# Two experts' token rows gathered by one indirect transfer and transposed together

## The reference, cut to what matters

```python
weights = g_w[:, None] * softmax(top_vals)        # two experts of one group per token
eid = (g_sel[:, None] * 8 + top_idx).reshape(-1)  # 1024 assignments to 32 experts
...
hid = silu(xb @ w_gate[e]) * (xb @ w_up[e])       # xb: the normalised rows routed to expert e
y   = hid @ w_down[e]                             # 1024 -> 512 -> 1024
...
x = x + sum(y[dest] * weights)                    # back to the tokens
```

## Time and profile before

| | us |
|---|---|
| median of 3 runs | 2028.13 (2027.52 to 2030.19) |
| profiled execution, its own time | 2028.83 |
| its span, first to last instruction | 2027.0 |
| expert matmuls, first and last (tiles large, xF) | 1535.9 and 1999.8 from the span's start |
| busy in the span: PE, DVE, ACT, POOL | 1924.9, 1053.2, 704.8, 57.3 |

### The profile page before, as it was taken

One profiled execution on the slowest core, in us unless ns is written; L12 is line 12 of the kernel. 1 busy time (PEld: TensorE's weight loads), 2 busy tenths in 40 slices (PEclk: granted clock), 3 DMA queues, 4 the chain that ended last, 5 costly groups with the idle time before them and its releaser, 6 DMA issues.

```text
span 2027.0 us, 22190 instructions
## 1 busy us (share of the span) xinstructions
PE 1924.9 (95%) x8902; PEld 1392.4 (69%) x8902; DVE 1053.2 (52%) x1686; ACT 704.8 (35%) x1150; POOL 57.3 (3%) x81
## 2 busy tenths in 40 slices
PE   7999999997999989999999999999998999999997
PEld 6888888775878767888888878877675444444443
DVE  5443544367667886544334446666764333332333
ACT  5321322345545354432222234665652111111111
POOL 0000000100000001000000000000001000000000
PEclk9999999998999999999999999999998999999999
DMA  6333332333222304333333333222189999999996
GB/s 176 95 89 106 96 94 84 71 78 54 70 67 68 109 22 133 95 94 94 94 104 94 94 94 94 76 61 57 32 295 384 406 403 400 406 409 409 409 412 260
DMA packets 260639, 338.92 MB, mean 167 GB/s; under 512 B 10305, under 2 KB 224321, under 8 KB 236977
## 3 DMA queue, kind: packets, MB, share of 16 engines
q1 hardware_dynamic: 254496, 322.28, 46.9%
q0 software_dynamic: 6032, 15.15, 2.2%
HBM read 333.00 MB, written 8.39 MB: 168 GB/s over the span
## 4 chain that ended last, share of the span: by engine, by line
PE 72%; DMA 13%; DVE 9%; ACT 5%; issue 1%; SPq 0%; DVEq 0%; POOLq 0%; ACTq 0%
PE bank L182 70%; DMA large<-w_up 10%; PE bank L185 2%; DMA stage<-w_in 1%; ACT wH L188 1%; ACT p L188 1%; DVE PTL L194 1%; ACT T L188 1%; DVE y L194 1%; DMA xg<-token_rows,tok 1%; DMA stage<-w_r 1%; DVE p L197 1%; DVE score L218 0%; DVE score L200 0%; DVE top L215 0%
## 5 line engine op out<-in xcount | busy, mean ns | idle before, releaser
L182 PE MATMUL bank<-hH,wH 128*128 128x512 f32 x1104 | 438.2, 397 | 21.0 <-DVE stage0L L194 12.0
L182 PE MATMUL bank<-hL,wH 128*128 128x512 f32 x1104 | 431.8, 391 | 0.0
L188 ACT ACTIVATE wH<-stage 128x1024 fp32r<-128x1024 f32 (+3 forms) x238 | 232.5, 987 | 113.0 <-PE bank L182 83.7
L182 PEld LDWEIGHTS bank<-hH,wH 128*128 128x128 f32 x1104 | 209.0, 189 | 68.3 <-DVE stage0L L194 12.0
L182 PE MATMUL bank<-large,xF 128*64 128x512 f32 x1024 | 235.6, 602 | 15.4 <-DMA large<-w_up 14.6
L182 PEld LDWEIGHTS bank<-hL,wH 128*128 128x128 f32 x1104 | 208.9, 189 | 44.3 <-issue 1.9
L182 PEld LDWEIGHTS bank<-large,xF 128*64 128x64 f32 x1024 | 75.0, 138 | 146.4 <-issue 127.8
L182 PE MATMUL bank<-hidH,wH 128*128 128x512 f32 x352 | 137.5, 391 | 2.1 <-DVE stage2L L194 0.9
L182 PE MATMUL bank<-hidL,wH 128*128 128x512 f32 x352 | 137.1, 389 | 0.0
L182 PE MATMUL bank<-large,hF 128*64 128x512 f32 x512 | 116.9, 598 | 1.9 <-DVE hF L194 1.9
L194 DVE TENSOR_TENSOR yoL<-bank,yoH 64x512 fp32r<-64x512 f32 x64 | 44.1, 689 | 110.2 <-ACT yoH L188 109.2
(11 more groups left out here) (480 smaller groups left out, 3356.3 us busy)
## 6 DMA issues: line engine op xcount, KB each, us to landing
large<-w_gate SPq DMA_DIRECT2D x64, 1024.0 KB, 26.9
large<-w_up SPq DMA_DIRECT2D x64, 1024.0 KB, 27.8
large<-w_down SPq DMA_DIRECT2D x64, 1024.0 KB, 27.8
stage<-w_in SPq DMA_DIRECT2D x58, 512.0 KB, 4.3
stage<-w_gate SPq DMA_DIRECT2D x44, 512.0 KB, 3.8
stage<-w_up SPq DMA_DIRECT2D x44, 512.0 KB, 3.7
stage<-w_down SPq DMA_DIRECT2D x16, 512.0 KB, 3.8
gates<-gt POOLq DMA_DIRECT2D x16, 256.0 KB, 4.0
```

The lines of the kernel that those rows point to most:

```text
L182: return self.e.matmul(*a, **k) if self.e is not None else Nothing()
L188: return self.e.activation(*a, **k) if self.e is not None else Nothing()
```

## The change

Gathers are made for two experts at once. The index table has 128 rows and one column for a pair: rows 0 to 63 are the even expert's tokens, rows 64 to 127 the odd expert's. The spare blocks keep a table of their own, `M.tokx`. One indirect DMA fills all 128 partitions of a gather buffer; there are two such buffers instead of three, and only the second waits for `ei` on its first use. A new step `turn_pair` makes eight transposes of 128 by 128 into two PSUM banks (2 and 4), where `turn_x` made eight of 64 by 128 for one expert into bank 2. DVE multiplies by the gain in two operations, one for each bank, and `xF` is kept for four experts. The fetch and the turn of a pair stand at the even `n`; the memory of the third gather buffer is taken by the second `xF` buffer. Weight loads and their order are not edited.

```diff
-        NGR = 3
+        NGR = 2
...
-            M.tok = sb([BLK, NB + NX], I32, "tok")
+            M.tok, M.tokx = sb([128, NB // 2], I32, "tok"), sb([BLK, NX], I32, "tokx")
...
-            for slot in M.xg.slots:
-                slot[1] = ("ei",)
-            M.xF2 = sb([128, 2, 8, BLK], F32, "xF")
-            M.xF = [M.xF2[:, k, :, :] for k in range(2)]
+            M.xg.slots[1][1] = ("ei",)
+
+            late_xF = sb([128, 2, 8, BLK], F32, "xF")
+            M.xF2 = [sb([128, 2, 8, BLK], F32, "xF"), late_xF]
+            M.xF = [M.xF2[k][:, e, :, :] for k in range(2) for e in range(2)]
...
-                add(Step("turn_x", n=n, xg=xg[n], bank=banks.take(("xT", n), 2)))
+                if n < NB:
+                    add(Step("turn_pair", n=n, xg=xg[n], banks=[banks.take(("xT", n, c), at) for c, at in enumerate((2, 4))]))
+                else:
+                    add(Step("turn_x", n=n, xg=xg[n], bank=banks.take(("xT", n), 2)))
...
-            for n in range(2, 2 + NGR):
-                fetch(n)
+            for p in range(1, 1 + NGR):
+                fetch(2 * p)
...
-                if 0 < n < NB - 2:
+                if n % 2 == 0 and 0 < n < NB - 2:
                     turn_x(n + 2)
-                if n + 2 + NGR < NB:
-                    fetch(n + 2 + NGR)
+                    if n + 2 + 2 * NGR < NB:
+                        fetch(n + 2 + 2 * NGR)
...
                 if n == 0:
                     turn_x(2)
+                    fetch(2 + 2 * NGR)
...
+                    if s.kind == "turn_pair":
+                        pe.wait_ge(*after("xg%d" % s.xg.at, n))
+                        rows = s.xg.t[:, :].rearrange("s (c p k) -> s c p k", c=2, k=4)
+                        for c in range(2):
+                            free(s.banks[c])
+                            for k in range(4):
+                                t = pe.transpose(s.banks[c].t[:, 128 * k:128 * k + 128], rows[:, c, :, k], mat("ident"))
+                            t.then_inc(*did("mm", "xT", n, c))
...
-                        pe.wait_ge(*(after("xT", n) if n >= 2 else after("xT", 0, s.i)))
+                        pe.wait_ge(*(after("xT", n) if n >= NB else after("xT", n - n % 2, s.i)))
...
-                then(dve.tensor_copy(M.tok[:, :], tf), "tok")
+                for half in range(2):
+                    then(dve.tensor_copy(M.tok[BLK * half:BLK * half + BLK, :], tf[:, half:NB:2]), *([] if half == 0 else ["tok"]))
+                then(dve.tensor_copy(M.tokx[:, :], tf[:, NB:]), "tokx")
...
+                    if s.kind == "turn_pair":
+                        dve.wait_ge(*after("gain_in", 7))
+                        if n >= 4:
+                            dve.wait_ge(*after("mm", "gu", n - 3, 1, 1))
+                        for c in range(2):
+                            dve.wait_ge(*after("mm", "xT", n, c))
+                            dve.tensor_tensor(M3.xF2[n // 2 % 2][:, :, 4 * c:4 * c + 4, :].rearrange("p e k n -> p k e n"),
+                                              s.banks[c].t[:, :].rearrange("p (k e n) -> p k e n", k=4, e=2),
+                                              gain2[:, 4 * c:4 * c + 4].unsqueeze(2).unsqueeze(3).broadcast_to([128, 4, 2, BLK]), ALU.mult).then_inc(*did("xT", n, c))
...
                     if s.kind == "fetch":
-                        pool.wait_ge(*after("tok",))
+                        K, ids = (128, M3.tok[:, n // 2:n // 2 + 1]) if n < NB else (BLK, M3.tokx[:, n - NB:n - NB + 1])
+                        pool.wait_ge(*after("tok" if n < NB else "tokx",))
...
-                        pool.indirect_dma_start(out=s.xg.t[0:BLK, :], out_offset=None, in_=h_rows[:, :],
-                                                in_offset=bass.IndirectOffsetOnAxis(ap=M3.tok[:, n:n + 1], axis=0),
+                        pool.indirect_dma_start(out=s.xg.t[0:K, :], out_offset=None, in_=h_rows[:, :],
+                                                in_offset=bass.IndirectOffsetOnAxis(ap=ids, axis=0),
```

More of the change, by code:

```diff
@@ L1271, in moe @@
             for k, s in dict(lg=[4, 36], gm=[4], a4=[4, 4], oh=[4, 4], oo=[2, 4, 32], m8=[8, 32],
-                             v1=[4], v2=[4], gw=[4], vm=[4], ct=[32], nx=[32], cx=[32], on=[32], dx=[32], ps=[4, 32],
-                             e8=[8], d8=[8], c8=[8], j8=[8], J=[8, 64]).items():
+                             v1=[4], v2=[4], gw=[4], vm=[4], ct=[32], nx=[32], on=[32], dx=[32], ps=[4, 32],
+                             e8=[8], d8=[8], c8=[8], j8=[8], J=[8, 64], cx=[32]).items():
                 M.R[k] = sb([128] + s, F32, k)
@@ L1280, in moe @@
             M.lgT = M.R["J"][0:36, :, :].rearrange("p a b -> p (a b)")
-            assert place[0] <= rows_at + 4096 * NGR, place[0] - rows_at
+            assert place[0] <= rows_at + 4096 * NGR + 4096
             b = dense(steps, ("router",), wcols("w_r", 0, 128), 8, h, ("lgT",), "norm")
@@ L1336, in fetch @@
             def fetch(n):
-                xg[n] = M.xg.take(("mm", "xT", n))
+                xg[n] = M.xg.take(("mm", "xT", n, 1) if n < NB else ("mm", "xT", n))
                 add(Step("fetch", n=n, xg=xg[n]))
             def turn_x(n):
-                add(Step("turn_x", n=n, xg=xg[n], bank=banks.take(("xT", n), 2)))
+                if n < NB:
+                    add(Step("turn_pair", n=n, xg=xg[n], banks=[banks.take(("xT", n, c), at) for c, at in enumerate((2, 4))]))
+                else:
+                    add(Step("turn_x", n=n, xg=xg[n], bank=banks.take(("xT", n), 2)))
             def of(n, name, c):
@@ L1775, in expert_steps @@
                     n = s.n
-                    if s.kind == "turn_x":
+                    if s.kind == "turn_pair":
[6 more added lines that the diff above has]
+                            t.then_inc(*did("mm", "xT", n, c))
+                    elif s.kind == "turn_x":
                         pe.wait_ge(*after("xg%d" % s.xg.at, n))
@@ L1790, in expert_steps @@
                             for j2, u in enumerate(s.units):
-                                t = pe.matmul(s.bank.t[BLK * j2:BLK * j2 + BLK, :], xF[n % 2][:, 4 * s.i + j, :], u.F[:, j, :],
+                                t = pe.matmul(s.bank.t[BLK * j2:BLK * j2 + BLK, :], xF[n % 4][:, 4 * s.i + j, :], u.F[:, j, :],
                                               start=s.i == 0 and j == 0, stop=s.i == 1 and j == 3)
@@ L2356, in moe_stage @@
                             for k in range(4):
-                                t = act.activation(M.xF2[:, :, 4 * c + k, :], s.banks[c].t[:, 128 * k:128 * k + 128].rearrange("p (e n) -> p e n", e=2),
+                                t = act.activation(M.xF2[0][:, :, 4 * c + k, :], s.banks[c].t[:, 128 * k:128 * k + 128].rearrange("p (e n) -> p e n", e=2),
                                                    ACT.Copy, scale=col("norm2", 4 * c + k))
@@ L2957, in expert_steps @@
                         dve.wait_ge(*after("gain_in", 7))
-                        dve.tensor_tensor(xF[n % 2], s.bank.t[:, :].rearrange("p (k n) -> p k n", k=8), wide(gain2[:, :], [128, 8, BLK]), ALU.mult).then_inc(*did("xT", n))
+                        dve.tensor_tensor(xF[n % 4], s.bank.t[:, :].rearrange("p (k n) -> p k n", k=8), wide(gain2[:, :], [128, 8, BLK]), ALU.mult).then_inc(*did("xT", n))
                     elif s.kind == "turn_hid":
```

## The result

| | before | after |
|---|---|---|
| median (5 runs each) | 2028.77 us | 2016.34 us (2015.80 to 2019.97) |
| ratio after / before | | 0.9933, 95% interval 0.9920 to 0.9947 |
| profiled execution, own time / span | 2028.83 / 2027.0 | 2015.80 / 2013.9 |
| last `w_up` that PE waits for has landed | 1992.7 | 1976.3 |

Lines of the page of the changed kernel, for rows 1: PE's busy time, then DMA and GB/s in the 40 slices.

What follows compares the result with a forecast made beforehand. The prediction took the experts' weight loads on DMA as the bound. PE, DVE and POOL counted 0 and DMA -1.5 us, taking the median from 2028.1 to 2026.6 us, with a given range of 2021.5 to 2031.5.

Steps and rivals of the forecast that it cites:

- The bound: Expert stage: weight loads set the end, 31.50 us per pair against PE's 28.67, with at least five loads queued.
- PE, DVE, POOL: Expert stage: PE's 0.84 us less per pair, DVE's operations and POOL's issue time all hidden beside loads, each counted 0.
- The gathers' disturbance: Weight loads beside gathers: 0.55 us lost per gather, 16.5 in all; 15 fewer instructions save 1.5 us, bounds 0 and 3.0.
- Rival A: Gathers: the loss belongs to the instruction, so halving their number saves 8.2 us, giving 2019.9; chance 0.08.
- Rival B: Expert stage: PE is the bound after all, so all 12.6 us come off, giving 2015.5; chance 0.05.
- Rival C: Gathers: more rows per transfer disturb weight loads more, adding 12.0 us, giving 2040.1; chance 0.05.
- Rival D: Tail: PE idles longer and its clock falls, costing 3.0 us for 16 matmuls, giving 2031.1; chance 0.03.
- the marks set for the next profile: Late stretch: the forecast expected a rate of 409 to 412 GB/s and a period of about 31.3 us.

Runs made afterwards that it cites:

- split64: Changed kernel with each pair's gather made as two transfers of 64 partitions, the second issued after the first landed; ratio to before 1.0003.
- twice: Changed kernel with every transpose of a pair made twice, 16 of 128x128 in place of 8; ratio to before 0.9922.
- split32: Changed kernel with a pair's gather made as four transfers of 32 partitions, each waiting for the one before; 2041.66 us, ratio to before 1.0044.
- split128: Like split64, but both transfers address 128 partitions, the other expert's 64 rows out of bounds and skipped; ratio to before 0.9953.
- split32b: split32 without the waits between its four transfers; ratio to before 1.0010.
- split64b: split64 without the wait between its two transfers; ratio to before 1.0013.
- wide1: Kernel before, with each of its 30 one-expert gathers addressing 128 partitions, rows 64 to 127 skipped; ratio to before 0.9982.
- after2: Changed kernel run again unedited, on the chip of warm and split32; ratio to before 0.9915.
- warm: Changed kernel with idle transposes of the identity filling PE's waits in the tail; 2016.62 us, ratio to before 0.9923.

## Why the prediction was wrong

**The bound** was read rightly. The end follows the landing of the loads; split64 has the changed kernel's PE work and the old time, twice has more PE work and the new time; PE's waits for `w_up` were there before and after. The five or more loads queued ahead covered every delay but the 13.6 us of split32.

**PE, DVE, POOL** counted 0, and were 0. PE's saving for a pair was 1.40 us in the period (28.67 to 27.27), not 0.84: eight transposes of 128x128 take 0.95 us in the chain where 1.36, twice the 0.68 of four, had been taken for them. That makes 2.20 - 0.95 = 1.25; the other 0.15 is not explained. Behind the loads it makes no difference. PE's waits for `w_up` did not grow by 12 us between 1805 and 1965, since both sides of the race became faster, PE by 1.40 us in a pair and the loads by 1.0; over the whole stage they grew from 14.6 to 18.8 us.

**The gathers' disturbance** is the step that failed. Its size was about right: 0.55 us for one, 16.5 us in all, and 16.4 came back at the last awaited load, 18.2 counted from the start of the stage. The step was "Halving the number of instructions saves half of that, 8.2 us, if the loss belongs to the instruction, and nothing if it belongs to the rows. Single gathers decide between the two". Single gathers of one form could only show that the loss grows with the rows. They could not show that it would stay when the form changes, and the change altered the form: 128 partitions in place of 64. The loss was 16.5 us for the 3.9 MB of rows in one form and nearly nothing in the other. So the saving was 16.4 us or more and not 1.5, and the upper end of 8.2 was not an end at all: the whole of the measured loss was the honest bound, as no row of before showed a gather of 128 partitions.

**Rival A** has the right sign and the wrong mechanism, as split128 and split32b show; it came within 4 us of the median. **Rival B** gave 2015.5, within 1 us of the median, and is refuted by twice, split64 and split64b: the nearest number had the wrong cause. **Rival C** is refuted by the rate. **Rival D**, the clock, came true beside the forecast rather than in place of it: waits of 2.4 and 1.95 us in the tail, +1.7 us on 16 matmuls each, 3.4 in all where 3.0 had been put. Only the first of these waits is new; the second was there before and cost nothing then, so why the clock fell behind it is open. Of the marks set for the next profile, "a late rate near 415 and a period below 31" was A's; the rate was 420, over every case, and the period 30.5.

## What to carry to other kernels

Where transfers are the bound, read the rate with and without each side stream, and take the whole difference as what a change of that stream's form may give back; that it scales with bytes or rows within one form says nothing of another form. Address side transfers to all 128 partitions, and fill both halves: wide1 shows that widening with skipped rows restores the rate (419) but leaves the DMA share near a half at the end, and 0.18% of gain where full halves give 0.67%. Work taken off an engine that waits for loads is worth nothing, and can cost a little when the clock falls behind one of its last waits.

## What the runs showed of the hardware

- A gather to 64 or 32 partitions beside 1 MB loads held the rate at 401 to 411 GB/s; one to 128 partitions with the same rows left it at 419 to 420, and at 415 late in wide1, where only half of each transfer held rows. From 1600 to 1760 the loads' own packets took 2.48 to 2.49 us of all 16 engines for each MB beside the narrow form and 2.40 to 2.41 beside the wide one.
- An indirect transfer of 128 rows landed 8.2 us after its issue, one of 64 rows after 7.2, and one addressed to 128 with only 64 of them valid after 8.2 to 8.3 (split128, wide1). With the valid rows always in the lower 64 (wide1), the DMA share fell to 0.47 from 1982 to 1994.
- The length of a wait alone does not say whether the clock falls. Sixteen matmuls took 5.17 to 5.35 us behind waits for a load of 4.06 (at 1825 in the changed kernel), 2.38, 2.35 (after2, split32) and 2.34 us (split32b), but 3.65 behind 2.89 and 2.34 (changed kernel, in the steady part), 2.84 (split32), 2.71 (split64b), 2.35 (split64) and 1.93 (twice). Behind the same wait of 1.95 us for DVE in the tail they took 3.65 before and 5.33 to 5.35 in every other kernel but warm, which fills it.
